# Products taken ahead of the norm: x times its feature gain goes through the next weight slab, the inverse root is applied behind PSUM (three of six norms of a fused two-block layer stack)

## What is computed

```python
for l in range(2):
    mod = c_act @ w_ada[l] + b_ada[l]
    sh1, sc1, gt1, sh2, sc2, gt2 = split(mod, 6)
    h = rms_norm_2(x, norm1[l]) * (1.0 + sc1) + sh1          # "norm 1"
    proj = h @ w_in[l]                                       # first columns: q
    ... retention, gating, pooling, branches -> merged
    x = x + gt1 * (merged @ w_out[l])
    h2 = rms_norm_2(x, norm2[l]) * (1.0 + sc2) + sh2         # "norm 2"
    hidden = jnp.square(jax.nn.relu(h2 @ w_ff1[l]))
    x = x + gt2 * (hidden @ w_ff2[l])
return rms_norm_2(x, final_norm)
```

## Time and profile before

| What | us |
|---|---|
| Median of three runs | 2777.82 |
| The runs | 2777.82, 4490.74, 2771.78 |
| The profiled execution | 2772.3 |
| Its span | 2770.5 |
| PE busy | 2693.5 (97%) |
| DVE, ACT, POOL busy | 1492.1, 1072.2, 906.2 |

### The profile page before, as it was taken

How to read it: one execution, slowest core, us unless ns; L and a number is a source line. 1 busy time by engine, 2 the same in 40 slices (tenths; PEclk the granted TensorE clock), 3 DMA queues, 4 the chain that set the end, 5 groups by cost and what they waited for, 6 DMA issues and landing times.

```text
span 2770.5 us, 33644 instructions
## 1 busy us (share of the span) xinstructions
PE 2693.5 (97%) x13510; PEld 2261.1 (82%) x13510; DVE 1492.1 (54%) x1630; ACT 1072.2 (39%) x1242; POOL 906.2 (33%) x209
## 2 busy tenths in 40 slices
PE   7899989999999999999999999999999999999998
PEld 6688678888789888888878888798988888888887
DVE  5764663899772455345363454644393364445435
ACT  3332362778542542334232223324433343323223
POOL 2221002000043244344433444341443444434434
PEclk9899898999989999999999999999999999999999
DMA  7110003799522265223233333221562233233333
GB/s 273 61 46 16 1 22 138 269 368 363 214 88 92 74 245 186 89 93 127 92 104 124 114 122 128 88 92 61 187 256 90 91 114 106 91 129 114 114 125 111
DMA packets 61145, 361.42 MB, mean 130 GB/s; under 512 B 7265, under 2 KB 8161, under 8 KB 25825
## 3 DMA queue, kind: packets, MB, share of 16 engines
q1 hardware_dynamic: 58720, 353.84, 35.7%
q10 hardware_dynamic: 2304, 5.90, 0.6%
HBM read 357.59 MB, written 2.10 MB: 130 GB/s over the span
## 4 chain that ended last, share of the span: by engine, by line
PE 81%; DVE 3%; ACT 1%; issue 1%; ACTq 0%; DVEq 0%
PE pd L266 19%; PE pd L267 19%; PE pd L268 19%; PE pd L287 2%; PE pd L286 2%; PE pd L285 2%; PE pd L1953 2%; PE pd L1955 2%; PE pd L1954 2%; DVE sb_y_lo L1683 2%; PE pd L1980 1%; PE px L323 1%; PE pd L1982 1%; PE pd L1981 1%; PE pd L1910 1%
## 5 line engine op out<-in xcount | busy, mean ns | idle before, releaser
L220 POOL TENSOR_TENSOR sb_w_lo<-sb_raw,sb_w_hi 128x2048 fp32r<-128x2048 f32 x182 | 850.1, 4671 | 1741.5 <-ACT sb_w_hi L211 1741.5
L266 PE MATMUL pd<-sb_h_hi,sb_w_hi 128*128 128x512 f32 x1664 | 662.6, 398 | 14.6 <-DVE sb_h_lo L423 10.0
L267 PE MATMUL pd<-sb_h_lo,sb_w_hi 128*128 128x512 f32 x1664 | 652.3, 392 | 0.0
L268 PE MATMUL pd<-sb_h_hi,sb_w_lo 128*128 128x512 f32 x1664 | 652.0, 392 | 0.0
L211 ACT CAST sb_w_hi<-sb_raw 128x2048 fp32r<-128x2048 f32 x182 | 347.9, 1912 | 391.3 <-PE pd L268 365.7
L266 PEld LDWEIGHTS pd<-sb_h_hi,sb_w_hi 128*128 128x128 f32 x1664 | 315.8, 190 | 85.2 <-issue 18.0
L266 PE MATMUL pd<-sb_y_hi,sb_w_hi 128*128 128x512 f32 x928 | 363.8, 392 | 8.3 <-DVE sb_y_lo L1683 4.2
L267 PEld LDWEIGHTS pd<-sb_h_lo,sb_w_hi 128*128 128x128 f32 x1664 | 316.0, 190 | 66.4 <-issue 2.2
L268 PEld LDWEIGHTS pd<-sb_h_hi,sb_w_lo 128*128 128x128 f32 x1664 | 315.2, 189 | 66.6
L267 PE MATMUL pd<-sb_y_lo,sb_w_hi 128*128 128x512 f32 x928 | 362.1, 390 | 0.0
L268 PE MATMUL pd<-sb_y_hi,sb_w_lo 128*128 128x512 f32 x928 | 361.9, 390 | 0.0
(11 more groups left out here) (541 smaller groups left out, 3869.4 us busy)
## 6 DMA issues: line engine op xcount, KB each, us to landing
sb_raw<-in_slabs SPq DMA_DIRECT2D x190, 1024.0 KB, 4.9
sb_moe_raw<-in_moe SPq DMA_DIRECT2D x56, 1024.0 KB, 6.5
sb_raw<-in_moe SPq DMA_DIRECT2D x28, 1024.0 KB, 6.4
sb_QK<-in_ada SPq DMA_DIRECT2D x32, 512.0 KB, 5.7
sb_V<-in_ada SPq DMA_DIRECT2D x32, 512.0 KB, 5.6
sb_M<-in_ada SPq DMA_DIRECT2D x16, 512.0 KB, 13.9
sb_Y<-in_ada SPq DMA_DIRECT2D x16, 512.0 KB, 5.9
sb_MG<-in_ada SPq DMA_DIRECT2D x16, 512.0 KB, 6.0
```

The costliest lines, as they stand in the source:

```text
L220: pool.tensor_tensor(w_lo[j][:], raw[j][:], w_hi[j][:].bitcast(F32), ALU.subtract).then_inc(w_lo_ready[j], 1)
L266: pe.matmul(out, w_hi[j][:, cols], hi[:, k], start=(k == 0), stop=False)
L267: pe.matmul(out, w_hi[j][:, cols], lo[:, k], start=False, stop=False)
L268: last = pe.matmul(out, w_lo[j][:, cols], hi[:, k], start=False, stop=(k == KT - 1))
```

## The change

For the three norms, the first slab behind the norm no longer takes h. While x is finished, ACT writes xT times the feature gain in rounded form (`raise_scalar`), DVE the remainder of it (`raise_vector`), into y_hi and y_lo, or for u = 4 into x_hi and x_lo, which lie over V and QK. PE goes on with the slab behind the norm at once; the token sums stand behind its tile 1, the spreading behind its tile 2, and behind tile 5 the product of the same slab with the shift vector in two parts (`shift_products`, 32 matmuls of two columns). DVE makes h as before, but behind that, and then multiplies the slab's result with the inverse root (`ahead_product`); ACT adds the shift's product as a bias where it leaves the slab. The other slabs take h as before. The first feed-forward group stands written out in front of the loop.

```diff
@@ slabs_to_x (PE): behind the last slab @@
+            slab_starts(pe, m + 2, 0)
+            for k in range(KT):
+                pe.wait_ge(ahead_lo, 8 * (u - 3) + k + 1)
+                slab_piece(pe, 0, k, *raised)
+                if k == 1:
+                    last_sums(pe, u, sq)
+                elif k == 2:
+                    spread_inverse(pe, u)
+                elif k == 5:
+                    shift_products(pe, u - 3)
...
+        def shift_products(pe, e):
+            pe.wait_ge(shift_ready, e + 1)
+            for f in range(2):
+                for k in range(KT):
+                    cols = slice(k * SLAB_COLS + f * P, k * SLAB_COLS + f * P + P)
+                    out = px[1][:, 2 * f:2 * f + 2]
+                    pe.matmul(out, w_hi[0][:, cols], shift_parts[:, k], start=(f == 0 and k == 0), stop=False,
+                              skip_group_check=True)
+                    last = pe.matmul(out, w_lo[0][:, cols], shift_parts[:, k], start=False, stop=(k == KT - 1),
+                                     skip_group_check=True)
+            last.then_inc(shift_done, 1)
+        def raise_scalar(act, tiles, into, gain):
+            for k in tiles:
+                act.activation(into[:, k], xT[:, k], ACT.Identity, scale=gain(k)).then_inc(ahead_hi, 1)
+        def raise_vector(dve, e, tiles, hi, lo, gain):
+            for k in tiles:
+                dve.wait_ge(ahead_hi, 8 * e + k + 1)
+                dve.scalar_tensor_tensor(lo[:, k], xT[:, k], gain(k), hi[:, k].bitcast(F32), ALU.mult,
+                                         ALU.subtract).then_inc(ahead_lo, 1)
+        def ahead_product(dve, v, m, e):
+            v(dve.tensor_copy(T[:, 2], px[3][:]))
+            dve.wait_ge(shift_done, e + 1)
+            dve.tensor_reduce(shift_out[:, 0:2], px[1][:, 0:4].rearrange("p (f n) -> p f n", f=2), AX.X, ALU.add)
+            dve.wait_ge(slab_done[0], m + 1)
+            for f in range(2):
+                dve.tensor_tensor(T[:, f], pd[f][:], T[:, 2], ALU.mult).then_inc(ahead_out, 1)
@@ slabs_to_x_scalar (ACT): behind slab n - 1, in front of its squares @@
                     act.wait_ge(slab_out[(n - 1) % 2], m + (n - 1) // 2 + 1)
+                    if raised is not None:
+                        raise_scalar(act, (2 * n - 2, 2 * n - 1), raised, gain)
                     norm_squares(act, sq, [n - 1])
@@ norm_hi_part (ACT) @@
             for k in range(KT):
+                if k == KT - 1 and slab_behind is not None:
+                    split(act, slab_behind, 0)
                 act.wait_ge(norm_val, 8 * u + k + 1)
@@ the feed-forward's first slab on ACT; layer 1's q slab does the same into QK with Identity @@
+        def y_raised(act, e, yb, vb):
+            for f in range(2):
+                act.wait_ge(ahead_out, 2 * e + f + 1)
+                ins = act.activation(T[:, f], T[:, f], ACT.Relu, bias=shift_out[:, f:f + 1])
+            ins.then_inc(slab_out[0], 1)
@@ DVE, the product that ends in x (with w_out; the last feed-forward group likewise) @@
+                shift_vector(dve, v, 2 * l, lay[:, MOD + 24:MOD + 32])
                 for n in range(4):
                     add_to_x(dve, v, L + L_WOUT + n // 2, n % 2, 4 * (n // 2), MOD + 16,
                              half=2 * l + 1 if n == 3 else None)
                     if n == 2:
                         norm_add(dve, 3 + 2 * l, O, 4 * l + 4)
+                    raise_vector(dve, 2 * l, (2 * n, 2 * n + 1), y_hi, y_lo, lambda k: lv_(GAIN + 8 + k))
                 norm_vector(dve, v, 3 + 2 * l, O, lambda k: lv_(GAIN + 8 + k), lambda k: lv_(MOD + 24 + k))
+                ahead_product(dve, v, L + L_FF, 2 * l)
```

More of the change, by code:

```diff
@@ L347, in norm_add, with slabs_to_x @@
                 dve.wait_ge(norm_added, added - 2 + n)
-        def slabs_to_x(pe, m, hi, lo, ready, u, sq, added):
+        def slabs_to_x(pe, m, hi, lo, ready, u, sq, added, raised=None):
             for n in range(3):
@@ L385, in slabs_to_x_scalar @@
             act.activation(sq[:, 6], xT[:, 6], ACT.Square).then_inc(half_sq, 1)
+            if raised is not None:
+                raise_scalar(act, (6,), raised, gain)
             act.preload_act_table(ACT.Sqrt)
@@ L388, in slabs_to_x_scalar @@
             act.activation(sq[:, 7], xT[:, 7], ACT.Square).then_inc(norm_sq, 1)
-            norm_roots(act, u)
+            if raised is None:
+                norm_roots(act, u)
+            else:
+                raise_scalar(act, (7,), raised, gain)
             act.copy(by_half(w_hi[1], 1), by_half(raw[1], 1)).then_inc(w_hi_ready[1], 1)
+            if raised is not None:
+                norm_roots(act, u)
         def by_half(buffer, f):
@@ L1606, in build @@
         hidT_lo = [over(f"hidT_lo{n}", T, 2 * TOK + 256 * n, [P, 256], F32R)[:] for n in range(2)]
+        x_hi, x_lo = (over(name, base, 0, [P, KT, TOK], F32R) for name, base in (("x_hi", V), ("x_lo", QK)))
         pos_row = T[:, 3]
@@ L1670, in y_scalar @@
                 act.copy(y_hi[:, bass.ds(2 * n + f, 1)], T[:, tj + f:tj + f + 1]).then_inc(y_hi_ready, 1)
+        def y_raised(act, e, yb, vb):
[3 more added lines that the diff above has]
+            ins.then_inc(slab_out[0], 1)
+            for f in range(2):
+                act.wait_ge(y_val, vb + f + 1)
+                act.copy(y_hi[:, f], T[:, f]).then_inc(y_hi_ready, 1)
         def y_vector(dve, v, m, j, value, n, yb, vb, tj=None, wait=None):
@@ L2023, in _, with rows @@
                 yb = Y_LAYERS + Y_PER_LAYER * l
-                def rows(at, hi, lo, ready=None):
-                    for n in range(4):
-                        slab_rows(pe, L + at + n // 2, n % 2, hi, lo, ready if n == 0 else None)
+                def rows(at, hi, lo, ready=None, begin=0):
+                    for n in range(begin, 4):
+                        slab_rows(pe, L + at + n // 2, n % 2, hi, lo, ready if n == begin else None)
                 def branch(at, y_at):
@@ L2033, in branch @@
                         slab_rows(pe, L + at + i, 1, y_hi, y_lo)
-                rows(L_Q, h_hi, h_lo, (h_ready, 8 * (2 * l + 2)))
+                rows(L_Q, h_hi, h_lo, (h_ready, 8 * (2 * l + 2)), 1 if l else 0)
                 for n in range(4):
@@ L2329, in _ @@
                 for n in range(4):
-                    plain(L + n // 2, n % 2, 2 * n, scale=1.0 if n < 2 else RET_SCALE, split_yet=n > 1)
+                    if n == 0 and l:
+                        for f in range(2):
+                            act.wait_ge(ahead_out, 2 * (2 * l - 1) + f + 1)
+                            ins = act.activation(QK[:, f], T[:, f], ACT.Identity, bias=shift_out[:, f:f + 1])
+                        ins.then_inc(slab_out[0], 1)
+                    else:
+                        plain(L + n // 2, n % 2, 2 * n, scale=1.0 if n < 2 else RET_SCALE, split_yet=n > 1)
                     if n == 0:
-                        split_next(act, L, 1)
+                        if not l:
+                            split_next(act, L, 1)
                         angle_tables()
@@ L2655, in _ @@
                 norm_vector(dve, v, 2 + 2 * l, O, lambda k: lv_(GAIN + k), lambda k: lv_(MOD + k))
+                if l:
+                    ahead_product(dve, v, L, 2 * l - 1)
                 dve.wait_ge(tables_loaded, 32 * l + 32)
@@ L2845, in up_down @@
                     dve.wait_ge(mod_stored, FF_GROUPS * l + q + 1)
+                    raised = last_group and l + 1 < LAYERS
+                    if raised:
+                        v(dve.tensor_tensor(next_mod[:], b_ada[:, ADA_COLS * (l + 1):ADA_COLS * (l + 1) + ADA_FIRST],
+                                            mod[:, 0:ADA_FIRST], ALU.add))
+                        v(dve.scalar_tensor_tensor(next_mod[:, 8:16], next_mod[:, 8:16], 1.0, v2[:, l + 1, 0:8],
+                                                   ALU.add, ALU.mult))
+                        shift_vector(dve, v, 2 * l + 1, next_mod[:, 0:8])
                     for n in range(4):
```

72 lines of the change are left out of this document (52 added, 20 removed).

## The result

The changed kernel takes 2800.15 us (median of four runs, 2792.67 to 2803.36), the kernel before 2774.80 (median of four, with one outlier of 4490.74). The ratio, which leaves the outlier out, is 1.0094, 95% interval 1.0062 to 1.0127: slower by some 26 us, less than 2%. It was forecast slower by 9, 2781.5, in a range up to 2792.

A forecast was written before the change was run, and what follows sets the result against it. PE, busy 97% of the span, was taken to bound the kernel. Gain -7.4, stall +9.9, w_lo wait +2.7 and clock +4 gave +9.2 on 2772.3, so 2781.5 us, in a range of 2767 to 2792.

The forecast's parts named there:

- The sign: Whole kernel: the change makes it slower, by 9.2 us.
- the mechanisms on DVE, POOL and ACT: Around each norm: POOL's splits hold DVE's remainders and eighth h_lo; at u = 4 ACT's tables and w_lo come later.
- The gain to be had, 7.4 us: PE's three spans at u = 3, 4, 5: 20.3 us of work against 22.0, 23.0 and 23.2, together 7.4 less.
- The stall, 9.9: In front of tile 6's square: PE idle 3.3 us at each of three norms, as POOL holds DVE's remainders.
- The first rival (not held): Remainders in front of tile 6 are not held by POOL: stall 1.3 at each norm, 2768.8 us; chance 0.22.
- The wait for w_lo at u = 4, 2.7: In front of slab 3 at u = 4: PE idle about 2.7 us, once, waiting for w_lo.
- The shift's matmuls at 0.114: Inside the slab: 32 two-column matmuls at the one-column pass's 0.114 us each, 3.6 in all.
- the second rival: At each norm: PE's clock falls twice, six falls, 12 us in place of 4, time 2789.5; chance 0.15.
- The room of 0.7 in front of slab 2: Behind the first slab at all three norms: slab 0's banks are free 0.7 us before PE needs them.
- the term "The clock": Behind the stall: PE's clock falls at two of three places, about 2 us each, 4 us.

The follow-up runs named there:

- all three edits: Changed kernel with remainders of tiles 4 and 5 behind tile 7's addition, sums in three times eight, shift's matmuls over tiles 3 to 6: 2767.64 us, ratio 0.9977.
- The kernel with the products first: Against all three edits, DVE's work on slab 0's banks (copy, reduction, two products) stands in front of the eighth h_lo: 2766.16 us, ratio 0.9981.
- the reorder: The kernel with the products first: DVE's work on slab 0's banks in front of the eighth h_lo, against all three edits: 2766.16 us, ratio 0.9981.
- two of 32: Changed kernel with only two of the shift's 32 two-column matmuls left at each norm: 2783.17 us, ratio 1.0038.
- first edit alone: Changed kernel with the remainders of tiles 4 and 5 moved behind tile 7's addition on DVE: 2779.43 us, ratio 1.0022.
- the sums apart: Changed kernel with the 24 one-column passes cut in three times eight, behind tiles 0, 1 and 2, spreading behind tile 3: 2792.64 us, ratio 1.0073.
- the 512 columns: Against first edit alone, the shift's 32 matmuls stream 512 columns in place of two: 2780.34 us, ratio 1.0024.
- the sums in one run again: Against the kernel with the products first, the 24 passes in one run behind tile 1, spreading behind tile 2: 2768.78 us, ratio 0.9985.
- four a tile: Changed kernel with the shift's 32 matmuls four behind each of tiles 0 to 5 and eight behind tile 6: 2799.97 us, ratio 1.0085.

## Why the prediction was wrong

The sign, the mechanisms on DVE, POOL and ACT and most terms came out. One term of the sum did not.

- **The gain to be had, 7.4 us: right.** The sum of PE's work in the span was 20.3 us; with no stall and no fall it measures 19.8 (all three edits, u = 3). The kernel with the products first takes 7.2 off at the three norms.
- **The stall, 9.9: right to 1.2 us.** 8.7 measured (2.90, 2.92, 2.92), because the first of the two remainders is held: 2.76 us in front of tile 6 against a median of 0.75. The first rival (not held) is out. The Trainium skill (SBUF — State Buffer, "Who interferes with whom") had said that a VectorE instruction with two SBUF inputs contends with a GpSimd instruction that reads SBUF, and this trace agrees.
- **The wait for w_lo at u = 4, 2.7: right.** 2.60 measured, its cause shown by the reorder that takes it to 0.67.
- **The shift's matmuls at 0.114: right**, 0.112 at full clock. That they bring the clock down was seen only in the second rival.
- **The room of 0.7 in front of slab 2** was there as long as the slab was long; with a shorter slab it was not (1.1 us with two of 32).
- **The step that failed is the term "The clock": "Taking the fall at two of three places: 4 us".** The clock fell at all three places behind the stall, and four times more inside the slab. By the trace the matmuls of 512 columns lose 14.6 us in seven falls (their number times 0.227 taken from the time they took: 2.8, 1.0, 2.5 at u = 3; 2.3, 1.4 at u = 4; 1.7, 2.9 at u = 5), and the few-column matmuls beside them 3.4 more (against 1.05 for tile 6's passes and the spreading, 2.73 for the sums, 3.6 for the shift's): 18.0. Put in the place of 4, with 8.7 for the stall and 2.6 for w_lo, the forecast's own sum gives -7.4 + 8.7 + 2.6 + 18.0 = 21.9; measured at the norms is 21.6. That it comes so near is partly luck, since the 7.4 itself is an estimate.

The mechanism had been named, in the second rival, with a chance of 0.15 and a condition: that 3 us of few-column passes alone bring the clock down. The runs show that they can, and that they do not always. The 32 two-column matmuls in one run (3.6 us) did so at seven norms of nine (two of three in the changed kernel, three of three with the first edit alone, two of three with the sums apart); the same 32 with 512 columns at none of three. The 24 passes in one run (2.73 us) did so at two of nine where no stall stands in front of them (first edit alone, the 512 columns, the sums in one run again), and at six of nine where one does (the changed kernel, two of 32, four a tile). Groups of 4 to 12 among full matmuls, with no wait beside them, began no fall in any kernel; behind a stall the half clock can run on through them. Why the same instructions lose the clock at one norm and keep it at another, these runs do not show. The rival was itself too small, since it counted two falls at each norm of 2 us and not those that run to 2.9.

The evidence against the rival was one row, the spreading of 1.16 at u = 3 of the kernel before. It was one of three, and the other two spoke the other way: at u = 4 and u = 5 of the same trace the spreading took 2.08, and at u = 5 the clock fell inside the sums (the rows stand in the section on the result). Read at all three norms, the trace of the kernel before would have given the rival a much larger chance.

The rest, from 21.6 to some 25, is the 3.9 from early in the program. It is in unchanged code, and what stands in front of u = 3 differs from execution to execution (-3.6 to +8.3 over all traces). Of the changed kernel's 3.9, 2.9 arise at the stretch of half clock shown in the last section, which one run had and the next had not. It is not put down to the change; whether a part of it is cannot be told from these runs.

## What to carry to other kernels

A busy PE is not a PE at full clock. When norm sums, spreading or small products are moved between full matmuls to fill the engine, count them as runs: cut runs like the ones here (24 and 32 matmuls, 2.7 and 3.6 us) into groups with full matmuls between. Before you set a chance by one row, read the same row at every place where the pattern recurs. A stall of 2.9 us on PE was worth 4.6 to 9.5 us here, 6.3 on average, so read the price of a wait as the wait and the half clock behind it. And behind any step that GpSimd can hold on VectorE, put nothing that PE waits for, if it can be helped: moving two remainders behind two additions took 14.5 us off at the norms.
